# Norm factors of three feed-forward stages brought to all partitions through a DRAM row

## What is computed

```python
x = x + 0.5 * swiglu(rms_norm(x, ffn1_norm[l]), w_gate, w_up, w_down)   # F = 2816
x = x + concat(diff_attention, conformer_conv, short_conv)(rms_norm(x, mix_norm[l]) @ w_in) @ w_out
x = x + cross_attention(rms_norm(x, xa_norm[l]), rms_norm(mem, mem_norm[l]))
x = x + 0.5 * swiglu(rms_norm(x, ffn2_norm[l]), w_gate, w_up, w_down)
```

```python
def rms_norm(x, g):
    return x * rsqrt(mean(x * x, axis=-1) + EPS) * g
def swiglu(h, w_gate, w_up, w_down):
    return (silu(h @ w_gate) * (h @ w_up)) @ w_down
```

## Time and profile before

| what | value |
|---|---|
| median of three runs | 1150.65 us (1150.36 to 1150.84) |
| profiled execution, span from the first to the last instruction | 1148.6 us |
| profiled execution, its own time | not given on the page |
| PE, DVE, ACT, POOL busy | 99%, 74%, 57%, 2% of the span |
| mean granted TensorE clock | 0.998 |
| moved by DMA | 210.92 MB |

### The profile page before, as it was taken

The page is one execution under the profiler, slowest core; times in us unless marked ns, Lnnn a source line. Parts: engine busy times, 40 slices in busy tenths (PEclk is TensorE's granted clock), DMA queues, the critical chain, the costliest instruction groups (busy, mean ns, idle before and its releaser), DMA issues.

```text
span 1148.6 us, 15684 instructions
## 1 busy us (share of the span) xinstructions
PE 1140.9 (99%) x6188; PEld 986.0 (86%) x6188; DVE 851.1 (74%) x1160; ACT 655.7 (57%) x937; POOL 21.6 (2%) x63
## 2 busy tenths in 40 slices
PE   9999999999999999999999999999999999999997
PEld 8888888888889888888888888888888888888886
DVE  7767667899867676666786676669998676766756
ACT  6555656547855564545565555564577556645444
POOL 1000000000000000000000000000000000000000
PEclk9999999999999999999999999999999999999999
DMA  8955654644444366555546656544535443656551
GB/s 283 321 202 177 206 155 177 220 150 176 156 166 160 112 225 206 179 190 194 194 153 241 204 181 195 191 165 166 183 147 205 162 147 122 227 176 204 174 190 62
DMA packets 66266, 210.92 MB, mean 184 GB/s; under 512 B 5009, under 2 KB 24209, under 8 KB 61073
## 3 DMA queue, kind: packets, MB, share of 16 engines
q1 hardware_dynamic: 65216, 209.26, 53.7%
q10 hardware_dynamic: 976, 0.66, 0.2%
HBM read 208.85 MB, written 1.05 MB: 183 GB/s over the span
## 4 chain that ended last, share of the span: by engine, by line
PE 95%; DVE 4%; DVEq 1%; issue 0%; ACT 0%
PE G L1658 28%; PE G L1662 15%; PE D L1526 10%; PE D L1527 10%; PE D L1528 10%; PE G L1619 3%; PE D L1619 3%; PE G L1526 3%; PE G L1528 3%; PE G L1527 3%; PE G L1625 2%; DVE w_lo L973 1%; PE D L1625 1%; DVE acc L1180 1%; PE D L1593 1%; DVEq L1182 1%
## 5 line engine op out<-in xcount | busy, mean ns | idle before, releaser
L973 DVE TENSOR_TENSOR w_lo<-w_raw,w_hi 128x2048 fp32r<-128x2048 f32 (+3 forms) x260 | 452.6, 1747 | 55.9 <-ACT w_hi L562 54.7
L562 ACT ACTIVATE w_hi<-w_raw 128x2048 fp32r<-128x2048 f32 (+3 forms) x260 | 382.0, 1478 | 41.8 <-PE G L1528 18.2
L1658 PE MATMUL G<-a,w_hi 128*128 128x512 f32 x1406 | 339.8, 390 | 0.0
L1658 PEld LDWEIGHTS G<-a,w_hi 128*128 128x128 f32 x1406 | 260.7, 188 | 52.9 <-issue 0.9
L1662 PEld LDWEIGHTS G<-a,w_lo 128*128 128x128 f32 x1406 | 184.2, 191 | 9.5
L1662 PE MATMUL G<-a,w_lo 128*128 128x256 f32 x1406 | 187.0, 282 | 0.0
L1077 DVE TENSOR_TENSOR zqk<-G,zqk 128x512 f32<-128x512 f32 x88 | 60.8, 691 | 153.1 <-ACT zqk L641 152.8
L641 ACT ACTIVATE zqk<-G 128x512 f32<-128x512 f32 x88 | 52.5, 596 | 180.2 <-PE G L1662 179.9
L1526 PE MATMUL D<-w_hi,hT_hi 128*128 128x512 f32 x352 | 138.2, 393 | 0.0
L1527 PE MATMUL D<-w_lo,hT_hi 128*128 128x512 f32 x352 | 137.9, 392 | 0.0
L1528 PE MATMUL D<-w_hi,hT_lo 128*128 128x512 f32 x352 | 137.0, 389 | 0.0
(11 more groups left out here) (259 smaller groups left out, 1273.5 us busy)
## 6 DMA issues: line engine op xcount, KB each, us to landing
w_raw<-w_dram SPq DMA_DIRECT2D x120, 1024.0 KB, 5.1
w_raw<-w_dram SPq DMA_DIRECT2D x143, 512.0 KB, 5.4
m_raw<-memT_dram SPq DMA_DIRECT2D x2, 1024.0 KB, 9.2
w_raw<-w_dram SPq DMA_DIRECT2D x6, 256.0 KB, 6.1
w_raw<-w_dram SPq DMA_DIRECT2D x8, 128.0 KB, 4.1
vx<-mem_dram SPq DMA_DIRECT2D x1, 1024.0 KB, 11.4
x<-x_dram SPq DMA_DIRECT2D x2, 256.0 KB, 4.9
gbc<-fin_dram SPq DMA_DIRECT2D x1, 512.0 KB, 7.8
```

Source lines behind the costliest of these rows:

```text
L562: A(w_hi[:, part(i)], w_raw[:, part(i)], ACT.Copy).then_inc(s_hi, 1)
L973: V.tensor_tensor(w_lo[:, part(i)], w_raw[:, part(i)], w_hi[:, part(i)].bitcast(F32), ALU.subtract).then_inc(s_lo, 1)
L1658: M(banks[b], whi[:, at:at + P], both, start=k == 0, stop=False)
```

## The change

Before the three later stages' factors were spread by diagonals and products; now ACT issues two transfers. The first writes `rinv` (128 x 2) to a row of 256 floats in DRAM, element by element. The second reads this row to each of the 128 partitions of `rinv_bc`. The wait for the factors and the first issue stand behind ACT's last high part of the input, ahead of the two weight splits. The wait for the first transfer and the second issue stand behind the weight splits, ahead of the tail copy of chunk 0. DVE's scaling of chunk 0 waits for the second transfer. The diagonals, the two products and the copy are gone from these stages.

```diff
+        rinv_d = nc.dram_tensor("rinv_scratch", (T,), F32, kind="Internal").ap()
...
+            def row_to_dram(l, f):
+
+                act.wait_ge(s_rinv, 4 * l + 3 * f + 1)
+                act.dma_start(rinv_d.rearrange("(t p) -> p t", p=P), rinv[:, :], allow_slow_non_contiguous=True
+                              ).then_inc(s_rrow, 16)
+
+            def row_to_all(l, f):
+
+                act.wait_ge(s_rrow, 16 * (2 * l + f))
+                act.dma_start(rinv_bc[:, :], rinv_d.rearrange("(a t) -> a t", a=1).to_broadcast([P, T])
+                              ).then_inc(s_rdma, 16)
...
                     norm_start(4 * l + 3 * f)
+                    row_to_dram(l, f)
                     split(l, stage, ("gu", 2, 0, 8))
                     split(l, stage, ("down", 0))
+                    row_to_all(l, f)
                     copy_tail(l, f, 0)
-                    broadcast(l, f)
                     silu(l, f, 0)
...
             def pair_scale(l, f, c):
 
-                if c == 0:
-                    dve.wait_ge(s_rbc, 2 * l + f + 1)
+                if (l, f, c) == (0, 0, 0):
+                    dve.wait_ge(s_rbc, 1)
+                elif c == 0:
+                    dve.wait_ge(s_rdma, 16 * (2 * l + f))
...
                     norm_lo(4 * l + 3 * f)
-                    rinv_diag(l, f)
                     split(l, stage, ("gu", 2, 0, 8))
...
-                if q:
-                    rinv_broadcast()
-
```

More of the change, by code:

```diff
@@ L288, in hymba_kernel @@
         s_rbc = sem("rinv_broadcast")
+        s_rrow = sem("rinv_in_dram")
+        s_rdma = sem("rinv_broadcast_by_dma")
         s_tail = sem("tail_copied")
```

## The result

The changed kernel takes 1174.27 us (1173.79 to 1175.03), the kernel before 1150.65 us (1150.36 to 1150.84): a ratio of 1.0206, 95% interval 1.0195 to 1.0217. It is slower by 23.6 us, outside the predicted range. The profiled span grew from 1148.6 to 1172.7 us.

A forecast was written before the change was run, and what follows sets the result against it. TensorE, busy 99% of the span, was taken to bound the kernel. Zero for products, DVE, copy and landings, plus 0 to 0.07 us a stage for the issue, gave 0 to +0.2, taken as +0.05: 1150.7 us, range 1149.7 to 1152.5.

The forecast's parts named there:

- The products leave TensorE: Ahead of chunk 2, removing two factor products gains 0, bound 0.23 us a stage, since chunk 2 waits for the pair sum.
- Rival 1: TensorE gets the removed products' 0.23 us a stage back, 0.69 us in all: 1149.95 us; chance 0.06.
- Diagonals and copy: Diagonals leaving DVE and the broadcast copy leaving ACT each gain 0; DVE idles instead, and TensorE needs chunk 0's hT_lo later.
- The issue: On ACT, issuing the first transfer costs 0.45 us, delaying weight splits by d = 0 to 0.45; TensorE at most 0.07 late.
- Landing of the first transfer: The row's write to DRAM, x, lands in 2.9 us (bounds 2.0 and 7.3), hidden in ACT's idle time; cost 0.
- The prediction's other estimate: For the first transfer, the skill's fixed DMA cost of some 2.0 us, mostly the write's receipt, leaving the sum unchanged.
- limit of 4.6 us: The first transfer's landing x from which ACT's tail copy of chunk 0 would be late.
- Rival 3: The first transfer's receipt holds ACT before the tail copy, from x = 4.6; 8.2 us at x = 7.3, 1158.85; chance 0.07.
- Landing of the second: The read into SBUF, y, lands in 3.4 us; hidden up to 4.8, the tightest user being chunk 3's weight remainder.
- Rival 4: 128 partitions reading one kilobyte of DRAM make y long, costing from 4.8; 7.5 us at 7.3, 1158.2; chance 0.05.
- Rival 2: The row's 256 elements cost as much as 4 KB pieces, x = 5.1: 1.6 us more, 1152.25 us; chance 0.05.
- Rival 5: Faster through something not seen: ACT's and DVE's freed time would have to pull TensorE forward; chance 0.02.

The follow-up runs named there:

- g2: Changed kernel with the write alone, each of the 256 4-byte elements in its own 64 bytes, scaling from another tile; one execution, 1151.03 to 1153.26 us with five others.
- k2: Changed kernel with the write alone, 256 4-byte elements as pairs packed in partition order, scaling from another tile; one execution, 1163.63 us.
- h5: Kernel with 128 elements of 8 bytes, TensorE finishing chunk 0 earlier and DVE's pair sum moved ahead of the first down block's low part; 1149.67 us, ratio 0.9990.
- j1: Kernel with 128 elements of 8 bytes in the write, its DRAM row shifted by 16 bytes; 1150.70 us, ratio 1.0003.
- h1: Kernel with 128 elements of 8 bytes in the write, its DRAM row shifted by 32 bytes; 1151.28 us, ratio 1.0003.
- e3: Changed kernel with only the second transfer, reading a row of the constants' input, no write and no wait on ACT; 1150.92 us, ratio 1.0004.
- e2: Changed kernel with only the first transfer and ACT's wait for it, the read left out, scaling from another tile; 1170.59 us, ratio 1.0171.
- h3: Kernel before, diagonals kept, with the slow 256-element write added and waited for only before chunk 6; 1150.57 us, ratio 0.9998.

## Why the prediction was wrong, point by point

- **The products leave TensorE: gain 0, bound 0.23.** Right. 0.07 us a stage was measured, and the new order gave the whole 0.23. Rival 1 was wrong for the change as it stands.
- **Diagonals and copy: gain 0.** Right: with neither transfer the ratio is 1.0005.
- **The issue: 0.45 us, d up to 0.45.** The issues take 0.38 and 0.34 us, and d was 0.13, since the first ran beside the a_hi copy.
- **Landing of the first transfer, x = 2.9 us, bounds 2.0 and 7.3.** This is the step that failed. Measured: 8.7, 9.7 and 10.1 us. I took the nearest row by size and queue, a load of 4 KB into SBUF, for a store of packed 4-byte elements to DRAM, and neither bound came from a row of that kind. The prediction's other estimate, near 2.0 us, did not help either: the same 256 elements took from 1.6 us (g2) to 10.1 us. That each element goes out by itself, which no row of the kernel before showed, the 272 packets bear out. The limit of 4.6 us could be tested only roughly: in every stage with x up to 4.8 us the tail copy was still released by TensorE (the runs of the write alone have no second issue behind the wait), and with x of 7.1 us and more (k2) by the transfer.
- **Rival 3** named the place and the waiter, at 0.07. At 7.3 us it gave 8.2 us. At the measured x its own formula, x less 4.6 in each stage, gives 4.1 + 5.1 + 5.5 = 14.7 us, against 13.1 us of late starts; the formula is some 0.5 us a stage too high, since the first issue began before the a_hi copy ended and the second took less than 0.45. The rest of the loss is two things it left out: the low clock after each stop (5.5 us) and the late scaling (4.5 us).
- **Landing of the second, y = 3.4, limit 4.8.** In the kernel with the fast write, y was 4.1 to 4.6 us at the same place; alone and early it was 2.8 to 2.9 us. The size was a little low. The limit held: y of 4.9 us (h5, j1) cost nothing, and in the third stage of h1 y was 5.9 us and TensorE stood for 0.51 us ahead of chunk 3, released by DVE's low part of its weights, the very user that the prediction named. Why y was 5.7 to 8.3 us in the changed kernel stays open in part (e3 above). Rival 4's reason, reading one kilobyte 128 times, is refuted.
- **Rival 2**, 256 pieces at the price of 4 KB pieces: refuted as a mechanism, since 256 separate elements land in 1.6 us.
- **Rival 5**, faster through something not seen: no run shows it in the change as it stands.

## What to carry to other kernels

A small transfer's landing cannot be taken from a transfer of the same size with another shape: before a chain is made to wait for one, measure the very shape, or choose a layout in which one element carries all that a partition has and the elements don't crowd (here 8 in 64 bytes instead of 16 took the write from some 9.7 to 3.1 us and the whole loss with it). Ask of removed work which wait takes its place; here it paid only once the order let the next product start. And price a stop of the bounding engine above its length: here 13.1 us of late starts brought another 5.5 us with them, since TensorE came back at half its clock.

## What the runs showed of the hardware that I had not expected

- Packed 4-byte elements to DRAM: 9.9 us for 1 KB and 9.4 us for 0.5 KB, while the same 256 elements spread by 64 bytes take 1.6 us.
- The 272 packets of such a write are over about two microseconds after the issue, as are those of the fast one (e2 and g2); the slow write lands more than 6 us after its last packet.
- Loads issued on another queue while such a write was under way were held up in the first stage: 11.2 and 12.7 us for weight loads that took 6.6 and 6.7 us (h3). In the second stage the same two took 7.0 and 8.1 us where they took 6.6 and 6.8, so how much is held up varies, and why was not tried.
- TensorE's granted clock fell from 1.00 to 0.50 during stops of 4.59 and 5.08 us and 1.4 us after one of 3.63 us, and stayed there for some 3.4 us in the first stage, 6.8 in the second and 3.4 in the third (windows of the changed kernel).
